# A gated linear recurrence inside a decoder trunk: the 64-row matmuls of two levels side by side, the gate products of both behind them

## The reference

```python
    def step(state, inp):                       # hgrn2_mixer, per chunk
        qt, kt, vt, lf = inp
        b = jnp.cumsum(lf, axis=2)
        o_inter = jnp.einsum('bhck,bhkv->bhcv', qt * jnp.exp(b), state)
        diff = b[:, :, :, None, :] - b[:, :, None, :, :]
        decay = jnp.exp(jnp.where(tri, diff, -jnp.inf))
        attn = jnp.einsum('bhtk,bhtsk,bhsk->bhts', qt, decay, kt)
        o_intra = jnp.einsum('bhts,bhsv->bhtv', attn, vt)
...
        gate = jax.nn.sigmoid(gates.reshape(B, S, N_BRANCH, D))   # gates: columns of h @ w_in
        merged = jnp.sum(gate * branch, axis=2)
```

## Time and profile before

| | us |
|---|---|
| median of three runs | 2239.13 (2235.25 to 2240.95) |
| the profiled execution | 2234.31 |
| its span, first to last instruction | 2232.5 |
| TensorE busy in the span | 2124.1 (95%) |
| recurrent levels of layer 1 of 2 | about 116, from 164 to 281 |
| the same in layer 2 | about 116, from 1267 to 1383 |

### The profile page before, as it was taken

How to read it: one execution, slowest core, us unless ns; L and a number is a source line. 1 busy time by engine, 2 the same in 40 slices (tenths; PEclk the granted TensorE clock), 3 DMA queues, 4 the chain that set the end, 5 groups by cost and what they waited for, 6 DMA issues and landing times.

```text
span 2232.5 us, 32746 instructions
## 1 busy us (share of the span) xinstructions
PE 2124.1 (95%) x12051; PEld 1703.5 (76%) x12051; DVE 1484.5 (66%) x2695; ACT 1010.4 (45%) x1867; POOL 381.1 (17%) x346
## 2 busy tenths in 40 slices
PE   7999999999899999999999999999998999999996
PEld 4897788787687786777679978888966878677774
DVE  4728766655767876777646487666367688377775
ACT  4523334554565325555435333345445643445551
POOL 2002200000001431444300021000000034124441
PEclk9999999999999999999999999999999999999998
DMA  9332233241325765766542222333222277446653
GB/s 315 95 88 62 81 119 95 77 120 55 89 93 183 267 240 222 276 250 248 189 150 88 81 81 85 102 110 105 77 70 81 81 257 270 201 158 240 244 211 121
DMA packets 196573, 333.71 MB, mean 149 GB/s; under 512 B 30528, under 2 KB 153280, under 8 KB 180416
## 3 DMA queue, kind: packets, MB, share of 16 engines
q1 hardware_dynamic: 169184, 305.33, 40.4%
q0 software_dynamic: 19296, 19.98, 2.8%
q10 hardware_dynamic: 7936, 6.30, 0.9%
HBM read 352.48 MB, written 51.38 MB: 181 GB/s over the span
## 4 chain that ended last, share of the span: by engine, by line
PE 76%; DVE 12%; ACT 5%; issue 3%; DMA 2%; POOL 0%; SPq 0%; POOLq 0%; DVEq 0%; ACTq 0%
PE ps L875 70%; PE ps L873 6%; DVE spare L2089 3%; DVE ring_rounded L2107 2%; ACT WH_rounded L1588 1%; DMA SQKV<-gate_logits 1%; DVE nmax L2344 1%; DVE SC L2717 1%; DMA Y<-y_rows 1%; DVE ps L2341 0%; DVE ssq L2274 0%; POOL M L3059 0%; DVE SC L2367 0%; DVE spare L2092 0%; DVE SQKV L2285 0%
## 5 line engine op out<-in xcount | busy, mean ns | idle before, releaser
L875 PE MATMUL ps<-X_rounded,WH_rounded 128*128 128x512 f32 x768 | 340.0, 443 | 16.4 <-DVE ring_rounded L2107 4.5
L2107 DVE TENSOR_TENSOR ring_rounded<-ring,WH_rounded 128x512 fp32r<-128x512 f32 (+2 forms) x190 | 234.6, 1243 | 132.8 <-ACT WH_rounded L1588 132.4
L875 PE MATMUL ps<-H_rounded,WH_rounded 128*128 128x512 f32 x768 | 301.4, 392 | 3.2 <-DVE SC L2717 3.0
L875 PE MATMUL ps<-X_rounded,ring_rounded 128*128 128x512 f32 x768 | 301.7, 393 | 0.0
L875 PE MATMUL ps<-WH_rounded,X_rounded 128*128 128x256 f32 (+1 forms) x960 | 274.8, 286 | 3.1 <-ACT TM L1800 1.0
L875 PE MATMUL ps<-ring_rounded,X_rounded 128*128 128x256 f32 (+1 forms) x960 | 271.3, 283 | 0.0
L875 PE MATMUL ps<-WH_rounded,H_rounded 128*128 128x256 f32 (+1 forms) x960 | 271.2, 282 | 0.0
L3059 POOL TENSOR_TENSOR M<-M,SC 128x512 f32<-128x512 f32 x48 | 79.5, 1670 | 947.0 <-DVE SC L2717 947.0
L1588 ACT ACTIVATE WH_rounded<-ring 128x512 fp32r<-128x512 f32 (+2 forms) x190 | 195.1, 1036 | 77.0 <-PE ps L875 65.5
L875 PEld LDWEIGHTS ps<-X_rounded,WH_rounded 128*128 128x128 f32 x768 | 144.9, 189 | 69.4 <-issue 27.9
L875 PEld LDWEIGHTS ps<-WH_rounded,X_rounded 128*128 128x128 f32 x960 | 184.4, 192 | 5.3 <-issue 2.4
(11 more groups left out here) (399 smaller groups left out, 4484.0 us busy)
## 6 DMA issues: line engine op xcount, KB each, us to landing
ring<-in_w_in SPq DMA_DIRECT2D x272, 256.0 KB, 4.0
Y<-in_moe_w_down SPq DMA_DIRECT2D x18, 1024.0 KB, 6.8
ring<-in_ada_w SPq DMA_DIRECT2D x64, 256.0 KB, 4.6
ring<-in_w_branch SPq DMA_DIRECT2D x64, 256.0 KB, 5.3
TM<-in_ada_w SPq DMA_DIRECT2D x14, 1024.0 KB, 10.0
DQK<-in_ada_w SPq DMA_DIRECT2D x14, 1024.0 KB, 9.2
ring<-in_moe_w_down SPq DMA_DIRECT2D x14, 1024.0 KB, 5.9
gate_logits<-CM SPq DMA_DIRECT2D x44, 256.0 KB, 2.7
```

Of the source, the lines that this page charges most:

```text
L875: ins = nc.tensor.matmul(o, lhsT, rhs, start=start, stop=stop)
L2107: ins = v.tensor_tensor(low[j][:, at:at + size], ring[:, j, at:at + size], high[i][:, at:at + size].bitcast(F32), ALU.subtract)
```

## The change

The loop body of `levels` is cut in two. The burst becomes a function `one(lv)`, called for two levels in a row, and the gate products of both follow. The state products, which were behind the gate products of level 4, are now behind those of level 5, since the outer loop variable is 4 for the pair of levels 4 and 5.

```diff
-                for lv in range(LEVELS + 1):
+                def one(lv):
+
                     if (pr, lv) == (3, LEVELS):
                         warm(3, 7)
...
                     if lv:
                         later(qk_used[i])
-                    gates("hgrn", pr * (LEVELS + 1) + lv, NT * (LEVELS + 1))
+
+                for lv in range(0, LEVELS + 1, 2):
+                    one(lv)
+                    one(lv + 1)
+                    for n in (lv, lv + 1):
+                        gates("hgrn", pr * (LEVELS + 1) + n, NT * (LEVELS + 1))
                     if lv == 4:
 
                         eng.wait_ge(emptied[2], p.so_far(emptied[2]))
```

## The result

The changed kernel takes 2308.64 us (median of four runs, 2305.81 to 2312.66), the kernel before 2237.19 (2233.18 to 2240.95): 1.0314 times as long, 95% interval 1.030 to 1.0328. It is slower, as forecast, but by 71 us where 53 were forecast, and the time lies 2.6 us above the range. The profiled execution took 2305.81 us (span 2304.1), 71.5 more than the one before.

The account below looks back on a forecast made before the run. TensorE, busy 95% of the span, was taken as the bound. Terms -9.6 + 24.3 + 6.6 + 9.0 + 14.4 = +44.7, plus 8 for the clock, raised 2234.3 to 2287.0; predicted 2290 us, range 2257 to 2306.

Parts of the forecast that it names:

- The saved passage: Between 64-row and 128-row matmuls on TensorE: two bursts side by side save 0.32 us, 30 times, 9.6 us.
- State products: Behind level 5's gate products: level 6's burst waits 3.75 us, or 3.14 in a layer's last head pair; +24.3 us.
- Level 7: Its burst directly behind level 6's waits about 1.1 us for its keys in three head pairs per layer: +6.6 us.
- Bank 3: Chunk ending in a pair's first level: the next gate product waits 0.9 us for ScalarE's copy, ten times; +9.0 us.
- Odd bursts of levels 2 to 5: With only the even burst ahead, odd bursts wait 1.8 us four times and 1.2 us six times: +14.4 us.
- the five pairs that were named: Per layer, pairs with chunk ends at n = 11, 17 (odd burst waits 1.8 us) and n = 2, 8, 26 (1.2 us).
- The six other pairs: Remaining pairs of levels 2 to 5 in both layers, taken as free; at 1.2 us each they would add 7.2.
- The clock: TensorE at half clock for 3.4 us behind each of eight new 3.75 us waits, 1.0 us cost each: +8 us.
- Only the two sure waits: Rival: only level 6's wait and bank 3 cost, odd bursts find their operands, clock stays up; 2258 us, chance 0.16.
- clock unmoved: Rival: all the forecast waits but no half clock, 2234.3 + 44.7 = 2279 us; chance 0.15.
- The saving wins: Rival: level 6's keys are ready when the state products end, only the passage saving counts; 2225 us, chance 0.03.
- Waits that feed each other: Rival: all odd bursts wait and slow clock delays the next feeding; 2300 us, 2305 beside the median, chance 0.05.

Follow-up runs that it names:

- the first experiment: The changed kernel with idle matmuls of some 3.5 us put into TensorE's wait between the state products and level 6's burst: 2292.87 us (1.0242).
- the second 27 us for 12: The kernel with idle matmuls behind the state products, plus 2 or 3 ahead of the waiting odd bursts of seven pairs per layer: 2286.16 us (1.0198).
- the kernel with one pair of levels 4 and 5 without ScalarE's order: Kernel before with only levels 4 and 5's bursts paired, state products at once behind them, ScalarE's copies not moved later: 2246.60 us (1.004).
- one pair in the right place: Kernel before with only levels 4 and 5's bursts paired, state products at once behind them, ScalarE's copies one step later: 2231.16 us (0.9954).

## Why the prediction was right and wrong

- **The bound and the direction.** TensorE's idle time is added in full: right. 69 of 71.5 us are in the two stages, which take 148.7 and 151.9 us where about 143 were forecast.
- **The saved passage, -9.6.** Right: 0.33 us for an idle matmul among gate products, and 0.33 from the changed kernel's own pair without a wait.
- **State products, +24.3.** Three waits of 3.67 and one of 3.07 us in the first stage, the same in the second: 28.2, less 4.4 that were there before, +23.8. Right, and the kernel with the state products behind the bursts shows that it is their place: 38 us come back with it, clock included.
- **Level 7, +6.6.** Where idle matmuls fill the wait for level 6 (the first experiment), it waits 0.5 us in the first head pair, 1.1 in the second and 2.1 in the third: 7.4 in both layers. In the changed kernel the first two vanish behind half clock, and the third stays. That three times 1.1 came out right as a sum is luck; only the second head pair, from whose rows it was read, waits 1.1.
- **Bank 3, +9.0.** Eight steps of 1.08 us and two at half clock of 1.12 and 1.30, where 0.23 is due: +8.8. Right.
- **Odd bursts of levels 2 to 5, +14.4.** Waits of 1.1, 1.3, 1.9, 1.9 and 1.2 us in each layer, in the five pairs that were named: 7.4 and 7.4. Right. The six other pairs ran free, as assumed.
- **The clock, +8: this step failed.** It put 3.4 us of half clock behind each of eight waits, 27 us in all, and 1.0 us as the cost of each. The stages show 61 us at 1.2 GHz, and they cost 23 us. The price for a us of half clock was not far off: 0.3 forecast, 0.4 measured on average (the first idle matmuls took away 34 us of half clock and gave back 11, the second 27 us for 12). The amount was wrong, in two ways. The larger one is the length of a slow stretch: 6.8 us at seven of the eight long waits, 51 us in all. The smaller one is that it counted only the long waits, while 10 us stand behind pairs of bursts whose odd one waits 1.1 to 1.9 us. The rows of the kernel before could have said both. From 861.84 TensorE idles 3.05 us in two pieces (1.67 and 1.38) with matmuls between them, and the clock of 0.65 over 9.76 us is 6.8 us at half clock; the same place of the other layer shows 6.8 us too. And the two rows that the step weighed against each other, 685.03 with half clock and 307.00 without, both came out the other way at the same place of the other layer. There the same instructions run behind nearly the same idle time (1.91 us, and 2.14 for 2.27):

```profile
861.84:871.60 9.76, 6.71 (x35) 6.52 (x35) 7.90 (x18) 0.00 (x0) 2.99 (x2) 0.65 0.17 52
1786.13:1791.73 5.60, 3.69 (x19) 3.13 (x19) 3.92 (x8) 5.57 (x8) 0.00 (x0) 1.00 0.90 311
1407.69:1414.25 6.56, 4.42 (x15) 3.78 (x16) 5.92 (x10) 2.60 (x6) 0.00 (x0) 0.74 0.95 303
```

So neither row was a rule, and an idle stretch of about 2 us can go either way. With the measured 23 in place of 8 the sum is 2234.3 - 9.6 + 24.3 + 6.6 + 9.0 + 14.4 + 23 = 2302, and the 2.7 us outside the stages and 1 us more are the rest of the profiled execution's 2305.8. The range was too short for the same reason: its upper end allowed 13.6 for the clock.

- **The rule of the Trainium skill** ("TensorE: Matmul & The Clock Gate", the table "Why this matters for your kernels") on long idle gaps held: half clock came at each of the eight waits of 3.07 to 3.68 us. It was row 307.00, set against it, that misled. The table's row names long idle gaps only; here half clock also came behind pairs with a wait below 2 us (state products behind the bursts, 0.92 and 0.95).
- **The rivals.** "Only the two sure waits" (2258) fell with the odd bursts' waits; "clock unmoved" fell with the clock column. "The saving wins" fell with the 3.67 us that level 6's keys come late. "Waits that feed each other" came nearest in time (2300 for the profiled execution) by a sum that did not happen: none of the further odd bursts waited, and its clock term of 13.6 was still too small.

What exactly decides whether a stretch of small matmuls and short waits is followed by half clock was not settled; the pairs of places in the two layers above show that the same instructions can go either way. In the order of before a wait of 1.04 us ahead of level 6 was followed by none, and in the kernel with one pair of levels 4 and 5 without ScalarE's order the first stage had one stretch of 6.8 us and the second, with the same waits, had none.

## What to carry to other kernels

Work that depends on nothing is cover for the chains beside it, and its place is worth more than a saved passage of the array: before putting two dependent bursts together, list for each engine in its own order what stands between the first burst and the second one's operands. A product that another engine waits for goes as early as it can (state products right behind the pair), and a copy goes behind an exponential that a burst waits for (ScalarE's copies one step later); with that alone the all-pairs order came from 71 us slower to 5, and one pair in the right place gained 0.5%. Cost a new wait on TensorE with the clock behind it: here waits worth 46 us net drew 61 us of half clock, which cost another 23. And before a row of the trace is taken for a rule, look at the same place in the other layer.

## What the runs showed that was not expected

- Half clock lasted 6.8 us behind a wait of 3.67 us, and up to 13.7 around the same wait where ScalarE's copies came later, though TensorE worked through most of it.
- Stages with no idle stretch of TensorE above 1.8 us had up to 20 us at half clock (state products behind the bursts); in the kernel with idle matmuls in all the long and middle waits they had none.
- The same instructions behind the same idle time were followed by half clock in one layer and by full clock in the other.
- Idle matmuls in a wait cost nothing that shows and brought the clock back: 88 more instructions per stage, and the two stages 23 us shorter together.
